# Start-up loads asked for by GpSimd in three steps, squares of the input added up by VectorE, other counts of idle matmuls, in a two-block transformer kernel

## The reference

```python
# start of the first block: norm, then one projection to 3088 columns
y = xf * lax.rsqrt(jnp.mean(xf * xf, axis=-1, keepdims=True) + EPS)
xn = (y * g).astype(x.dtype)
proj = xn @ w_in
...
log_a = jax.nn.log_sigmoid(gate_lr @ w_gate_up + b_gate) / GLA_GATE_TAU
...
x = x + concat([y_moba, y_gla]) @ w_out
hn = rms_norm(x, ffn_norm_g)
h = causal_dwconv(hn @ w_ffn_up, conv_w, conv_b)
x = x + (silu(h_gate) * h_val) @ w_ffn_down
```

## Time and profile before

| | |
|---|---|
| executions shown | 880.18, 876.56, 872.31 us; median 876.56 |
| profiled execution | 875.95 us, its span 874.1 us |
| TensorE busy | 859.3 us, 98% |
| VectorE, ScalarE, GpSimd busy | 709.1, 477.7, 101.2 us |
| moved by DMA | 191.68 MB, mean 219 GB/s |

### The profile page before, as it was taken

How to read it: one execution, slowest core, us unless ns; L and a number is a source line. 1 busy time by engine, 2 the same in 40 slices (tenths; PEclk the granted TensorE clock), 3 DMA queues, 4 the chain that set the end, 5 groups by cost and what they waited for, 6 DMA issues and landing times.

```text
span 874.1 us, 19335 instructions
## 1 busy us (share of the span) xinstructions
PE 859.3 (98%) x7326; PEld 833.8 (95%) x7326; DVE 709.1 (81%) x1109; ACT 477.7 (55%) x747; POOL 101.2 (12%) x134
## 2 busy tenths in 40 slices
PE   7999999999999999999999999999999999999996
PEld 6988899999999999999999999988999999999996
DVE  3898866889999978888889977888889998766552
ACT  4756576555555567444445567565645764444451
POOL 1031102000001540000002301000010200000021
PEclk6999999999999999999999999999999999999998
DMA  7453338566668984788889958655587568555651
GB/s 271 145 164 112 114 118 278 162 193 219 214 219 280 369 284 144 225 295 291 290 291 324 339 162 277 203 187 193 175 280 275 178 202 290 192 192 192 217 169 49
DMA packets 53384, 191.68 MB, mean 219 GB/s; under 512 B 5936, under 2 KB 6464, under 8 KB 53264
## 3 DMA queue, kind: packets, MB, share of 16 engines
q1 hardware_dynamic: 41760, 149.96, 51.3%
q0 software_dynamic: 10704, 39.20, 13.5%
q10 hardware_dynamic: 864, 1.73, 0.6%
HBM read 189.82 MB, written 1.05 MB: 218 GB/s over the span
## 4 chain that ended last, share of the span: by engine, by line
PE 91%; DVE 6%; ACT 1%; issue 1%; DMA 1%; DVEq 0%; SPq 0%; ACTq 0%
PE ps L396 27%; PE ps L397 26%; PE ps L398 26%; DVE w_lo L1320 2%; PE ps L487 1%; PE ps L489 1%; PE ps L488 1%; PE ps L563 1%; PE ps L620 1%; PE ps L509 1%; PE ps L594 1%; DVE ada_raw L1613 1%; DMA X<-x_in 1%; PE ps L580 0%; PE ps L602 0%
## 5 line engine op out<-in xcount | busy, mean ns | idle before, releaser
L1320 DVE TENSOR_TENSOR w_lo<-raw,w_hi 128x1024 fp32r<-128x1024 f32 (+1 forms) x282 | 339.8, 1221 | 76.1 <-ACT w_hi L915 75.3
L396 PE MATMUL ps<-xh,w_hi 128*128 128x256 f32 x1290 | 360.4, 279 | 0.7 <-DVE w_lo L1320 0.6
L397 PE MATMUL ps<-xl,w_hi 128*128 128x256 f32 x1290 | 357.1, 277 | 0.0
L398 PE MATMUL ps<-xh,w_lo 128*128 128x256 f32 x1290 | 357.1, 277 | 0.0
L915 ACT ACTIVATE w_hi<-raw 128x1024 fp32r<-128x1024 f32 (+1 forms) x282 | 288.6, 1050 | 94.2 <-PE ps L398 68.5
L396 PEld LDWEIGHTS ps<-xh,w_hi 128*128 128x128 f32 x1290 | 243.1, 188 | 3.7 <-issue 2.6
L397 PEld LDWEIGHTS ps<-xl,w_hi 128*128 128x128 f32 x1290 | 242.8, 188 | 0.3 <-issue 0.2
L398 PEld LDWEIGHTS ps<-xh,w_lo 128*128 128x128 f32 x1290 | 242.6, 188 | 0.0
L396 PE MATMUL ps<-act_hi,w_hi 128*128 128x256 f32 x528 | 146.6, 278 | 0.4 <-DVE act_lo L1605 0.4
L397 PE MATMUL ps<-act_lo,w_hi 128*128 128x256 f32 x528 | 146.5, 277 | 0.0
L398 PE MATMUL ps<-act_hi,w_lo 128*128 128x256 f32 x528 | 146.5, 277 | 0.0
(11 more groups left out here) (270 smaller groups left out, 1151.8 us busy)
## 6 DMA issues: line engine op xcount, KB each, us to landing
raw<-w SPq DMA_DIRECT2D x282, 512.0 KB, 4.3
ada_raw<-ada_w POOLq DMA_DIRECT2D x72, 512.0 KB, 4.9
X<-x_in SPq DMA_DIRECT2D x4, 256.0 KB, 5.4
out<-X SPq DMA_DIRECT2D x4, 256.0 KB, 2.4
tab<-tab_in ACTq DMA_DIRECT2D x1, 640.0 KB, 4.1
gmask<-gmask_in ACTq DMA_DIRECT2D x1, 512.0 KB, 5.4
cact<-c_in POOLq DMA_DIRECT2D x1, 512.0 KB, 6.5
bm<-bias_in POOLq DMA_DIRECT2D x1, 512.0 KB, 8.3
```

What stands on the lines that cost most here:

```text
L396: pe.matmul(o, lh, rh, start=start, stop=False, skip_group_check=True)
L397: pe.matmul(o, lh, rl, start=False, stop=False, skip_group_check=True)
L398: return pe.matmul(o, ll, rh, start=False, stop=stop, skip_group_check=True)
L1320: v.tensor_tensor(w_lo[:, slot(h), 0:n], raw[:, slot(h), 0:n], w_hi[:, slot(h), 0:n].bitcast(F32), ALU.subtract).then_inc(lo_ready, 1)
```

## The change

Six edits.

1. `w_glr` and `w_gup` are asked for by GpSimd once the first root is taken; `posi` and the first 768 columns of `tab` once all of `xn` is made; `gmask` and the two masks of `tab` once 6 halves of weights are used. ScalarE asks for `cols` alone. `gmask_landed` now counts two transfers.
2. VectorE adds the squares of tiles 2, 3 and 4, 5 onto 0, 1, and 7 onto 6. TensorE sums three tiles at the start instead of eight.
3. `keep_clock`: 6 wide ones (384 columns) instead of 4 at the start, 2 instead of 1 before the first projection and before the first feed-forward part; new are 2 narrow ones (128 columns) between sums and spread in `norm_start` and `norm_tokens`, and one wide one ahead of the last sum of the last norm.
4. In the first norm VectorE makes `xn` of tile 0 before the first weight split and tile 1 before the second. ScalarE makes the high part of the third half before the last group of `xh`. TensorE waits for the first half of the low parts only, and for the second where it is used.
5. In the last two convolution steps the second half of the weight split comes after `act_lo`.
6. In `raw_up` (the two SwiGLU parts) a half of a weight split comes before a pair of `xl`.

```diff
+IDLE_ENTRY = {0: 2, C_UP[0]: 2}
...
@@ block.gpsimd
+            pool.wait_ge(sd_done, 1)
+            pool.dma_start(b1["w_glr"][:, :], glr_in).then_inc(aux_landed, 16)
+            pool.dma_start(b1["w_gup"][:, :], gup_in).then_inc(aux_landed, 16)
+            pool.wait_ge(xt_ready, len(NEXT))
+            pool.dma_start(b1["posi"][:, :], pos_in.to_broadcast([P, S])).then_inc(pos_landed, 16)
+            pool.dma_start(tab[:, 0:TAB["causal"]], tab_in[:, 0:TAB["causal"]]).then_inc(tab_landed, 16)
+            pool.wait_ge(half_used, 6)
+            pool.dma_start(b1["gmask"][:, :, :], gmask_in).then_inc(gmask_landed, 16)
+            pool.dma_start(tab[:, TAB["causal"]:NTAB], tab_in[:, TAB["causal"]:NTAB]).then_inc(gmask_landed, 16)
...
@@ block.tensor
-            def keep_clock(bank, n):
+            def keep_clock(bank, n, w=3):
...
             def high_part_first(c, x_wait):
+                pe.wait_ge(lo_ready, 2 * c + 1)
                 pe.wait_ge(xh_ready, x_wait + 1)
                 for j, f in parts:
+                    if j and f == 0:
+                        pe.wait_ge(lo_ready, 2 * c + 2)
...
-                if not shifted:
-                    keep_clock(u % 2, IDLE_SPREAD)
-                pe.wait_ge(lo_ready, h + 2)
-                if not shifted:
+                if shifted:
+                    pe.wait_ge(lo_ready, h + 2)
+                else:
+                    keep_clock(u % 2, IDLE_ENTRY[c])
                     high_part_first(c, x_wait)
...
             def norm_start():
-                for k in range(KC):
-                    if k % 2 == 0:
-                        pe.wait_ge(sq_done, k + 2)
-                    m = token_sums(k, k == 0, k == KC - 1)
+                for j, k in enumerate((0, 1, 6)):
+                    if k != 1:
+                        pe.wait_ge(first_sum, 2 if k == 0 else 3)
+                    m = token_sums(k, j == 0, j == 2)
                 m.then_inc(ss_done, 1)
                 pe.wait_ge(consts_ready, 1)
+                keep_clock(0, 2, 1)
                 norm_spread(0)
...
-            def norm_tokens(n, q, added, tiles_left):
+            def norm_tokens(n, q, added, tiles_left, c, ahead=0):
+                pe.wait_ge(bank_free[bank_use(c) % 2], bank_use(c) // 2)
                 for j, k in enumerate(tiles_left):
+                    if k == 7:
+                        keep_clock(bank_use(c) % 2, ahead)
...
+                keep_clock(bank_use(c) % 2, 2, 1)
                 norm_spread(n)
...
-            keep_clock(0, IDLE - 2)
+            keep_clock(0, IDLE)
...
-            norm_tokens(6, 5, 24, (0, 7))
+            norm_tokens(6, 5, 24, (0, 7), C_UP[2] + FT, ahead=1)
@@ block.scalar
-            act.dma_start(b1["posi"][:, :], pos_in.to_broadcast([P, S])).then_inc(pos_landed, 16)
             act.dma_start(cols[:, :], cols_in).then_inc(cols_landed, 16)
-            act.dma_start(b1["w_glr"][:, :], glr_in).then_inc(aux_landed, 16)
-            act.dma_start(b1["w_gup"][:, :], gup_in).then_inc(aux_landed, 16)
...
             hi(0)
-            act.dma_start(tab[:, :], tab_in).then_inc(tab_landed, 16)
-            act.dma_start(b1["gmask"][:, :, :], gmask_in).then_inc(gmask_landed, 16)
-            norm_hi(0)
-            hi(1)
+            norm_hi(0, weights=1)
+            hi(1, halves=(1,))
@@ block.vector
                 rstd_tokens(n)
-                if n == 0:
-                    lo(0, halves=(1,))
                 dve.wait_ge(rstd_spread, n + 1)
                 for j, (k0, n_) in enumerate(NEXT):
                     ...
                     ins.then_inc(xt_ready, 1)
+                    if n == 0 and j < 2:
+                        lo(0, halves=(j,))
...
-                    if j:
+                    if j and not split_first:
                         lo(c + 2, i=i, halves=(1,))
...
                 v.tensor_tensor(al, av[:, vv, :], ah.bitcast(F32), ALU.subtract).then_inc(act_ready, 1)
+                if split_first:
+                    lo(c + 2, i=i, halves=(1,))
...
+                lo(c0 + 4, halves=(0,))
                 pair_lo(m, 2)
-                lo(c0 + 4, halves=(0,))
...
+            for j, (a, b) in enumerate(((slice(0, 2), slice(2, 4)), (slice(0, 2), slice(4, 6)), (6, 7))):
+                dve.wait_ge(sq_done, 4 + 2 * j)
+                if j == 1:
+                    dve.wait_ge(first_sum, 1)
+                v.tensor_tensor(xn[:, a, :], xn[:, a, :], xn[:, b, :], ALU.add).then_inc(first_sum, 1)
             dve.wait_ge(cols_landed, 16)
-            lo(0, halves=(0,))
```

More of the change, by code:

```diff
@@ L30 @@
 IDLE = 6
-IDLE_SPREAD = 1
 NEXT = [(0, 1), (1, 1), (2, 2), (4, 2), (6, 2)]
@@ L202, in build @@
         out_written = sem("out_written")
+        first_sum = sem("first_sum")
         block = ctx.enter_context(nc.Block())
@@ L398, in three @@
                 return pe.matmul(o, ll, rh, start=False, stop=stop, skip_group_check=True)
-            def keep_clock(bank, n):
+            def keep_clock(bank, n, w=3):
                 for _ in range(n):
-                    pe.matmul(ps[:, bank, 0:3 * P], mean[:, 0, :], mean[:, :, :].rearrange("p a n -> p (a n)"), start=True, stop=True)
+                    pe.matmul(ps[:, bank, 0:w * P], mean[:, 0, :], mean[:, 0:w, :].rearrange("p a n -> p (a n)"), start=True, stop=True)
             def feature_tile(c, h, kc, first, last, shifted=False):
@@ L782, in _ @@
             mix_ends(C_OUT1, b1["yh1"], b1["yl1"])
-            norm_tokens(1, 1, 2, (6, 0, 1, 7))
+            norm_tokens(1, 1, 2, (6, 0, 1, 7), C_UP[0])
             ffn_up(0, C_UP[0], 1)
@@ L960, in raw_hi, with norm_hi @@
                 f(xr_h[:, k, 0:S], X[:, k, :], ACT.Copy, scale=modA[:, sub, k:k + 1]).then_inc(xh_ready, 1)
-            def norm_hi(m):
+            def norm_hi(m, weights=None):
                 for j, k in enumerate(NEXT):
+                    if weights is not None and j == len(NEXT) - 1:
+                        hi(weights, halves=(0,))
                     act.wait_ge(xt_ready, scaled(m) + j + 1)
@@ L1550, in level_copy @@
                     dve.wait_ge(pool_zero, 2)
-                    dve.wait_ge(gmask_landed, 16)
+                    dve.wait_ge(gmask_landed, 32)
                 for i in range(1 if l == LEVELS else 2):
@@ L1567, in level_copy, with up_step @@
                         v.copy_predicated(dst, mask, src).then_inc(lv_copied, 1)
-            def up_step(conv, fi, c, j, i=0):
+            def up_step(conv, fi, c, j, i=0, split_first=False):
                 u = bank_use(c)
@@ L1623, in conv_up @@
                         for vv in range(2):
-                            up_step(True, 0, c0 + 2 + vv, 2 + vv, i=i)
+                            up_step(True, 0, c0 + 2 + vv, 2 + vv, i=i, split_first=n is None)
                     if n == 0:
```

## The result

The changed kernel takes 868.67 us (median of 16 runs, 867.02 to 876.36), the kernel before 873.84 on the same chip (16 runs, 870.60 to 880.32): ratio 0.9931, 95% interval 0.991 to 0.9953. The profiled execution took 869.38 us, its span is 867.5 instead of 874.1.

What follows compares the result with a forecast made beforehand. TensorE bounds the kernel, busy 859.3 of 874.1 us. Terms 2.7 + 0.35 + 0.4 + 0 + 0.2 = 3.65 us off 875.95 give 872.3; with 0.6 for the median, 872.9. Within 1%: 0.88; faster 0.08, slower 0.04.

Steps and rivals of the forecast that it cites:

- input earlier: Start: with three 128 KB loads moved to GpSimd, the input lands 0 to 0.96 us earlier; 0.95 taken.
- root at: Start, first norm: earlier input and fewer TensorE sums let the root begin at 9.7 instead of 12.11 us.
- first `xn` at: Start, VectorE: reciprocal directly after the root, spread ending at 11.7; `xn` of tile 0 starts then instead of 16.09 us.
- first product at: Start, TensorE: after two wide idle matmuls of 1.35 us each, first product at 14.4 instead of 17.17 us.
- second part earlier: First projection: the gain of the start reaching its second part, bounds 1.6 to 3.7 us by the clock; 2.7 taken.
- first feed-forward entry: Entry of the first feed-forward part: idle matmuls may keep the clock up; 1.1 gained to 1.6 lost, 0.35 us taken.
- convolution end: Last `act_lo` comes one split earlier, removing TensorE's 0.40 us idle: 0.4 us gained, at least 0.
- `raw_up`: SwiGLU parts, VectorE order changed: no TensorE idle time there, so 0 us gained.
- last norm: End: idle matmuls hold the clock, spread 0.71 instead of 1.11 us; 0.4 gained or 0.1 lost, 0.2 taken.
- I take 2.7, near the first: Start: clock rises 4.0 us after the first product as before, so nearly all of the 2.8 us stays.
- the clock does not fall: Rival, start: added idle matmuls keep the clock full, 3.7 us gained there, 871.0 us in all; chance 0.17.
- that scatter, not the cases, makes most of the range: Whole kernel: three executions lie 7.9 us apart, a median of a few can be 3 us off; cases lie within 1%.

Runs made afterwards that it cites:

- the kernel before, two more profiles: The kernel before, nothing changed, profiled in two more executions: 877.74 and 878.41 us.

## Why the forecast was right and wrong

| step | forecast | measured |
|---|---|---|
| input earlier | 0.95 | 0.73 to 0.75 (1.2 by the middle of 7 and 13 profiles) |
| root at | 9.7 | 9.71 |
| first `xn` at | 11.7 | 11.04 |
| first product at | 14.4 | 12.71 |
| second part earlier | 2.7 | 4.57 in this pair, of which 1.0 is given back by 48 us; by the middle of all profiles 3.3, of which 2.3 last to the convolution |
| first feed-forward entry | 0.35 | -0.1, none shown |
| convolution end | 0.4 | 0.6, and 2.2 more in some executions |
| `raw_up` | 0 | 6.1 where the long distance follows the gap: 3 of 6 profiles |
| last norm | 0.2 | 0.3 in this pair, none against the other profiles |

*Loads*: right, on the input as on the landings: 2.7 and 2.6 us for the gate weights, needed over 6 us later. The Trainium skill (DMA: Bandwidth & Descriptors, "Issuing engines are not separate DMA queues") would give the queue alone nothing. The runs agree as far as they go: with all but the gate weights asked for by ScalarE again, but behind the input, nothing was lost (868.39 us, last square at 7.41); what counted was that the requests came behind the input. The wait for `posi` (1.64 us) was free, as said.

*Start*: a second step failed here, "I take 2.7, near the first", with the reason that the same TensorE work stands before it. The clock did not fall at all: the rival "the clock does not fall" (0.17) is what happened. Its bound of 3.7 was too small for this pair of profiles: the two wide idle matmuls took 1.46 us together instead of 2.7, and the spread 0.71. I argued that sums and waits were the same as before; they were not, since VectorE's additions and the new order took away most of them. Undone one at a time, idle matmuls cost 1.7, order 1.2, loads 0.65, sums 3.6 us of the second part; of the median 1.5, 0.4, 0.7 and 2.3. That 2.3 us last to the convolution, near the 2.7 taken, is luck: the clock gave more than was forecast and part of it was lost again. So is the root at 9.71: the input came 0.2 later than forecast, and the sums, at the full clock, took less. The Trainium skill (TensorE: Matmul & The Clock Gate, "The HAM clock gate") has activity as what releases the clock; the trace agrees with it for dense work, while the one-column sums did not hold the clock.

*Given back*: 0.8 to 1.0 us up to 48 us. It goes with the race of a VectorE product with GpSimd's in all 20 profiles; no run turned the race round, so that it is the cause is not shown. In 13 profiles with loads by GpSimd it always ended 1.33 to 1.79; of 7 with none asked for by it early, 6 ended 1.88 to 0.68 and one, of the kernel before, as the others. Why those loads should tip it was not found.

*Last norm*: the forecast took the spread's 1.11 us as the price of the low clock. In the five other profiles with the last norm as before, the spread takes 0.71 without any added matmul, as here (the first of "the kernel before, two more profiles"):

```profile
869.73 0.71 PE L514 MATMUL ps<-ident,rstd_t 128*128 128x128 f32 x4 [0.55 <-DVE rstd_t L1331]
```

and from the last product to the end they take as long as the changed kernel (8.65 and 8.70 us). The term is worth nothing that shows.

*The step that failed most* is `raw_up`: "no TensorE idle time in its stretches, so nothing to win". The gap there is under 0.2 us wide, and little is won by its width. But the 163 us behind it took 6.1 us more in 3 of the 6 profiles with the gap, and with the old order alone put back 8 of 12 executions were long (median 874.77), against 2 of 27 of the changed kernel. With it failed the reading of the spread: "that scatter, not the cases, makes most of the range" took 7.9 us between three executions as a property of the measurement, where much of it was one of the kernel that this edit removes. The median of those three, 876.56, was also a poor base: 16 executions gave 873.84. Of the 5.2 us between the medians the sum had 3.65. Between executions that are not long the change is worth 3.8 (medians 872.3 of 78 and 868.5 of 25), by the profiles about 3.0: 2.3 of the start and 0.7 at the convolution's end. What makes the median move further is how rarely the changed kernel is long: 2 of 27 executions.

Open stay: what decides the distance at a gap, why it can change without one (near 553 us), and why the gap at 154 us, which all kernels have, drew the longer one in 2 of 20 profiles while the one at 703 us did it in 3 of 6.

## What to carry to other kernels

Where executions of a TensorE-bound kernel fall into groups some us apart, compare the count of equal matmuls over the same 20 us in two of them before calling it noise; then close the small gaps ahead of the longest dense stretches, however short, by bringing the operand they wait for one step forward. Idle matmuls kept the clock here only with short pauses around them, so time them together with the order of the other engines. One profile may be the slow one of its kernel: take two or three before pricing a term of under 1 us, such as the last norm here. A wait that a profile shows, as that for `posi`, may be free, and one that it shows no brackets for may cost 6 us.

## What the hardware showed beyond that

- 256-column matmuls in a dense stretch stand 0.1133 or 0.1178 us apart at a granted clock of 1.00, for up to 1517 of them; those of 258 columns stood at 0.120. Nothing else was seen to differ in the rows.
- With one-column sums, though TensorE was busy with them for 4.65 us without a break, the clock fell to 0.50 (at 10.5 us); in the changed kernel it stayed at 1.00 from 12 to 14 us with 1.04 us of busy time of 2. In one and the same kernel (before) the low stretch at the start lasted 13.7, 10.2 and 6.8 us in three executions.
- A two-operand product of 512 columns on VectorE took 0.68 us and GpSimd's beside it 1.88 when GpSimd's had started 0.03 to 0.04 us ahead (six profiles), and 1.78 to 1.81 against 1.30 to 1.34 when it had started 0.04 to 0.10 us ahead (fourteen).
- The requests of GpSimd at the start took 0.54 to 0.70 us of its time each, and 128 KB landed 2.6 to 4.8 us after them.
